# Experts of a mixed transformer step: 96 slots in plain fp32 over four column groups, in place of 128 slots in three split passes

## The reference

```
logits = (x @ w_router)                       # 8 experts
top_v, top_i = top_k(logits, 2); top_w = softmax(top_v)
gates = sum(one_hot(top_i, 8) * top_w[..., None], axis=1)
for e in range(8):
    y = y + gates[:, e:e+1] * ((silu(x @ we_gate[e]) * (x @ we_up[e])) @ we_down[e])
```

## Time and profile before

| | |
|---|---|
| median of three runs | 1605.54 us |
| the profiled execution's own time | 1617.21 us |
| its span, first to last instruction | 1615.4 us |
| TensorE busy | 1531.6 us, 95% |
| VectorE, ScalarE busy | 1133.4 us (70%), 977.0 us (60%) |
| mean granted clock | 0.953 of full speed |
| HBM read | 462.80 MB, 287 GB/s over the span |
| transfers of expert weights | 336 of 1 MB each |

### The profile page before, as it was taken

One profiled execution on the slowest core, in us unless ns is written; L12 is line 12 of the kernel. 1 busy time (PEld: TensorE's weight loads), 2 busy tenths in 40 slices (PEclk: granted clock), 3 DMA queues, 4 the chain that ended last, 5 costly groups with the idle time before them and its releaser, 6 DMA issues.

```text
span 1615.4 us, 23144 instructions
## 1 busy us (share of the span) xinstructions
PE 1531.6 (95%) x8380; PEld 1282.7 (79%) x8380; DVE 1133.4 (70%) x1260; ACT 977.0 (60%) x1131; POOL 30.5 (2%) x62
## 2 busy tenths in 40 slices
PE   7798699999797899999999999999999999999996
PEld 4755689999784878888888888888888888888885
DVE  1431634444514489989988989889989989988893
ACT  1422543344414367768777777777777777877771
POOL 0030000000030000000000000000000000000000
PEclk7898799999797899999999999999999999999997
DMA  9564567777543369989989989989989999998960
GB/s 346 196 215 141 176 242 274 275 275 247 176 158 110 116 227 361 365 327 360 363 326 357 373 316 365 365 317 359 369 313 375 365 337 345 363 371 312 363 247 28
DMA packets 210286, 464.99 MB, mean 288 GB/s; under 512 B 9226, under 2 KB 51892, under 8 KB 195892
## 3 DMA queue, kind: packets, MB, share of 16 engines
q1 hardware_dynamic: 208324, 462.80, 79.2%
q10 hardware_dynamic: 1904, 1.41, 0.3%
HBM read 462.80 MB, written 1.38 MB: 287 GB/s over the span
## 4 chain that ended last, share of the span: by engine, by line
PE 93%; DVE 4%; ACT 2%; issue 1%; DMA 0%; SPq 0%; DVEq 0%; ACTq 0%
PE ps L1515 13%; PE ps L1517 13%; PE ps L1516 13%; PE ps L1536 6%; PE ps L1538 6%; PE ps L1537 6%; PE ps L1272 5%; PE ps L1273 4%; PE ps L1274 4%; PE ps L1237 3%; PE ps L1482 2%; PE ps L1473 2%; PE ps L1283 2%; PE ps L1525 2%; PE ps L1215 1%; PE ps L1247 1%
## 5 line engine op out<-in xcount | busy, mean ns | idle before, releaser
L1036 DVE TENSOR_TENSOR low<-ring,high 128x1024 fp32r<-128x1024 f32 x672 | 795.5, 1222 | 78.4 <-ACT high L732 55.0
L732 ACT ACTIVATE high<-ring 128x1024 fp32r<-128x1024 f32 x672 | 697.5, 1061 | 163.3 <-PE ps L1517 105.1
L1515 PE MATMUL ps<-high,xg 128*128 128x512 f32 x896 | 358.7, 400 | 0.0
L1517 PE MATMUL ps<-high,xg 128*128 128x512 f32 x896 | 351.4, 392 | 0.0
L1516 PE MATMUL ps<-low,xg 128*128 128x512 f32 x896 | 348.2, 389 | 0.0
L828 DVE TENSOR_TENSOR low<-ring,high 128x1024 fp32r<-128x1024 f32 x102 | 121.2, 1222 | 153.1 <-ACT high L582 153.1
L1272 PE MATMUL ps<-hx,high 128*128 128x256 f32 x640 | 184.0, 288 | 28.9 <-DVE hx L869 13.5
L1517 PEld LDWEIGHTS ps<-high,xg 128*128 128x128 f32 x896 | 168.2, 188 | 39.4
L1516 PEld LDWEIGHTS ps<-low,xg 128*128 128x128 f32 x896 | 168.4, 188 | 35.5
L1515 PEld LDWEIGHTS ps<-high,xg 128*128 128x128 f32 x896 | 169.1, 189 | 32.1
L1273 PE MATMUL ps<-hx,high 128*128 128x256 f32 x640 | 182.0, 284 | 0.0
(11 more groups left out here) (200 smaller groups left out, 1294.5 us busy)
## 6 DMA issues: line engine op xcount, KB each, us to landing
ring<-in_moe_w_gate SPq DMA_DIRECT2D x112, 1024.0 KB, 7.1
ring<-in_moe_w_up SPq DMA_DIRECT2D x112, 1024.0 KB, 7.4
ring<-in_moe_w_down SPq DMA_DIRECT2D x112, 1024.0 KB, 6.9
ring<-in_w_ada SPq DMA_DIRECT2D x48, 1024.0 KB, 11.5
ring<-in_ffn_w_gate SPq DMA_DIRECT2D x11, 1024.0 KB, 10.0
ring<-in_ffn_w_up SPq DMA_DIRECT2D x11, 1024.0 KB, 5.4
ring<-in_ffn_w_down SPq DMA_DIRECT2D x11, 1024.0 KB, 7.2
ring<-in_w_in SPq DMA_DIRECT2D x8, 1024.0 KB, 9.6
```

What stands on the lines that cost most here:

```text
L732: A(high[:, (MP0 + i) % PIECES, :], ring[:, s, half * PIECE:(half + 1) * PIECE], ACT.Copy).then_inc(high_ready, 1)
L1036: V.tensor_tensor(low[:, q, :], ring[:, n % SLOTS, half * PIECE:(half + 1) * PIECE], high[:, q, :], ALU.subtract).then_inc(low_ready, 1)
L1515: mm(ps[:, bank, :], xh, hi[:, j, :], start=kk == 0, stop=False)
L1517: last = mm(ps[:, bank, :], xl, hi[:, j, :], start=False, stop=kk == KD - 1)
```

## The change

An expert gets 96 slots, three groups of 32, and is computed in plain fp32 without splits. The stationary operand is one group of 32 slots; the moving one is 512 weight columns; four such *units* go to the four column groups of the array. Hidden columns are worked in four steps of 1024, 1024, 1024 and 512, each as two halves (`E_WIDTH` 512, 512, 512, 256). With three groups and two halves there are six units for gate and six for up, twelve matmuls for each 128 rows of input. They fill banks 0, 1 and 2. Down gives twelve again (`DOWN`): even and odd hidden rows, two output halves, three groups, in banks 3, 4 and 5.

```diff
+CAP = 96
+ROUNDS = -(-N2 // CAP)
+E_WIDTH = (512, 512, 512, 256)
+E_COL = (0, 1024, 2048, 3072)
+UNITS = (tuple((0, u, u) for u in range(4)), tuple((1, u, u) for u in range(4)), ((0, 4, 0), (0, 5, 1), (1, 4, 2), (1, 5, 3)))
+DOWN = ((0, 0, 0, 3, 0), (0, 0, 1, 3, 1), (0, 0, 2, 3, 2), (0, 1, 2, 3, 3),
+        (0, 1, 0, 4, 0), (0, 1, 1, 4, 1), (1, 0, 2, 4, 2), (1, 0, 1, 4, 3),
+        (1, 0, 0, 5, 0), (1, 1, 1, 5, 1), (1, 1, 2, 5, 2), (1, 1, 0, 5, 3))
+TURN_BANK, GATHER_BANK = 6, 0
-COMBINE_BANKS = (6, 7, 3, 2)
+COMBINE_BANKS = (6, 7, 3, 4)
```

```diff
+ESLOTS = 14
+        ering = nc.alloc_sbuf_tensor_at("ering", [128, ESLOTS, SLOT], f32, offset=ring_at)
+                    k = 512 // width
+                    for half, w in enumerate((e_gate, e_up)):
+                        src = w[one, :, j * k:(j + 1) * k, E_COL[s]:E_COL[s] + 2 * width].rearrange("o p k n -> (o p) k n")
+                        sp.dma_start(to[:, half * SLOT // 2:(half + 1) * SLOT // 2].rearrange("p (k n) -> p k n", k=k), src).then_inc(arrives, 16)
```

TensorE's part, with its first round written out for the eight experts where it was a loop:

```diff
+                    def gate_up(s, j):
+                        i = E_ITEM["gu", s, j]
+                        width = E_WIDTH[s]
+                        rows = 512 // width
+                        w = arrived_e(i).rearrange("p (t r n) -> p t r n", t=2, r=rows)
+                        for r in range(rows):
+                            kk = j * rows + r
+                            for bank, units in enumerate(UNITS):
+                                for t, u, group in units:
+                                    c, g = divmod(u, 3)
+                                    last = mm(ps[32 * group:32 * group + 32, bank, 0:width], xg[:, kk, 32 * g:32 * g + 32], w[:, t, r, c * width:(c + 1) * width],
+                                              start=kk == 0, stop=kk == KD - 1)
+                        last.then_inc(pieces_used, 1)
+                    def turn(s):
+                        width = E_WIDTH[s]
+                        pe.wait_ge(eh_ready, k * NSTEP + (s + 1))
+                        for n in range(width // 128):
+                            a = n // 2 * 256 + n % 2
+                            nc.tensor.transpose(ps[:, TURN_BANK, n * 128:(n + 1) * 128], hm[:, 0, a:a + 255:2], ident)
+                            last = nc.tensor.transpose(ps[:, TURN_BANK + 1, n * 64:(n + 1) * 64], hm[0:64, 1, a:a + 255:2], ident[0:64, 0:64])
+                        last.then_inc(ehT_done, 1)
+                    wait_xg(k + (rnd + 1))
+                    for i, (what, s, j) in enumerate(EXPERT):
+                        if what == "gu":
+                            gate_up(s, j)
+                        else:
+                            down(s, j)
+                        if i + 1 == GATE_UP_END[0]:
+                            pe.wait_ge(Y_ready, k + (rnd + 1))
+                            combine(e)
+                            pe.wait_ge(acc_ready, k * 4 + (4 * rnd + 4))
+                            turn(0)
+                        elif what == "d" and s < NSTEP - 1 and j == 2 * E_WIDTH[s] // 256 - 1:
+                            turn(s + 1)
+                            if s + 1 == NSTEP - 1:
+                                gather(e + 1)
+                if rnd == 0:
+                    for e in range(NE):
+                        expert(e)
+                else:
+                    with pe.Fori(0, NE) as e:
+                        expert(e)
```

ScalarE takes silu in two parts (banks 0 and the first half of bank 2) and one of the two transposed blocks, VectorE multiplies in two parts and takes the other block, and neither splits anything. The six output parts of odd hidden rows are added on VectorE after ScalarE has copied two banks of even ones:

```diff
+            def add_Y(n):
+                dve.wait_ge(Y_even_ready, n)
+                V.tensor_copy(Y[64:96, 512:1024], ps[96:128, 3, :]).then_inc(Y_moved, 1)
+                dve.wait_ge(Y_moved, n)
+                for odd, half, g, bank, j in DOWN:
+                    if odd:
+                        y = Y[32 * g:32 * g + 32, 512 * half:512 * (half + 1)]
+                        last = V.tensor_tensor(y, ps[32 * j:32 * j + 32, bank, :], y, ALU.add)
+                last.then_inc(Y_ready, 1)
```

More of the change, by code:

```diff
@@ L47 @@
 FSTEPS = FF // FC
-EC = 512
-ESTEPS = FE // EC
 SLOTS = 7
@@ L482, in rest @@
                     load(e, i)
             def first_of_next(e, k):
-                for i in range(SLOTS):
-                    before = i + SLOTS * (PER_EXPERT[i] - 1)
-                    sp.wait_ge(low_ready, k * E_PIECES + (MP0 + 2 * (before + 1)))
+                for i in range(E_FIRST):
+                    sp.wait_ge(pieces_used, k * E_ITEMS + (MP0 + E_ITEMS + before_in_slot(i)))
                     load(e, i)
@@ L495, in experts @@
                 rest(NE - 1, rnd)
[L497 to L501, removed]
+            for i in range(E_FIRST):
+                if E_SLOT[i] < SLOTS:
+                    n = MOE0 + E_SLOT[i] - SLOTS
+                    if n >= N0:
+                        n -= SLOTS
+                    free(sp, n)
+                else:
+                    sp.wait_ge(pieces_used, MP0)
                 load(0, i)
@@ L506, in _ @@
             with sp.If(more > 0):
-                first_of_next(0, NE - 1)
-                experts(1)
+                for rnd in range(1, ROUNDS):
+                    first_of_next(0, NE * rnd - 1)
+                    experts(rnd)
             sp.wait_ge(y_first_ready, 1)
@@ L769, in expert @@
[L769 to L777, removed]
-                    take_Y()
[L779 to L789, removed]
@@ L1028, in _ @@
             mixer(1)
-            def split_e(k, a, z):
-                for i in range(a, z):
-                    n, half = divmod(i, 2)
-                    q = (MP0 + i) % PIECES
-                    dve.wait_ge(high_ready, k * E_PIECES + (MP0 + i + 1))
-                    V.tensor_tensor(low[:, q, :], ring[:, n % SLOTS, half * PIECE:(half + 1) * PIECE], high[:, q, :], ALU.subtract).then_inc(low_ready, 1)
-            split_e(0, 0, AHEAD)
             dve.wait_ge(logits_done, 1)
@@ new lines, in down @@
+                    def down(s, i):
+                        w = arrived_e(E_ITEM["d", s, i]).rearrange("p (r n) -> p r n", r=2)
+                        c, n = divmod(i, E_WIDTH[s] // 256)
+                        if i == 0:
+                            pe.wait_ge(ehT_first_ready, k * NSTEP + (s + 1))
+                            pe.wait_ge(ehT_last_ready, k * NSTEP + (s + 1))
+                        for odd, half, g, bank, group in DOWN:
+                            u = 3 * c + g
+                            h = (hT_first[:, 2 * n + odd, 32 * u:32 * u + 32] if u < 4 else hT_last[:, 2 * n + odd, 32 * (u - 4):32 * (u - 4) + 32])
+                            last = mm(ps[32 * group:32 * group + 32, bank, :], h, w[:, odd, 512 * half:512 * (half + 1)],
+                                      start=(s, i) == (0, 0), stop=(s, i) == (NSTEP - 1, 2 * E_WIDTH[s] // 256 - 1))
+                        last.then_inc(pieces_used, 1)
```

263 lines of the change are left out of this document (107 added, 156 removed).

## The result

The kernel after the change takes 1630.88 us (median of 4 runs, 1628.38 to 1638.16) against 1605.06 for the kernel before (4 runs, 1604.23 to 1608.98), measured beside each other: a ratio of 1.0163, with a 95% interval of 1.0126 to 1.0201. The forecast was 1573, so the change is slower by 25.8 us where 32 us less were expected. The profiled execution took 1629.55 us, with a span of 1627.7.

What follows compares the result with a forecast made beforehand. TensorE alone was taken to bound the expert stage: 120.9 us per expert against 125.87 gave -39.8, start -0.3, end +7.9, total -32 us, so 1573. The forecast by itself ranged 1561 to 1586, with rivals 1559 to 1622.

Steps and rivals of the forecast that it cites:

- Gather, combine, transposes: TensorE's small work per expert: gather 3.5 us, combine 3.3, 28 transposes 3.3 (1.6 to 3.3).
- changes of array layout: Joints where TensorE enters or leaves four column groups: eight per expert at 0.1 us more each, 0.8 (0.4 to 1.6).
- The streams: Gate, up and down matmuls of an expert: 107.9 us against 115.2, with narrow steps at 0.214 us.
- rival A: Narrow load and matmul pairs in the last gate/up step don't come fast enough, so slower: 1618 at the middle; chance 0.2.
- The waits: TensorE waiting for activation and additions: 1.9 us before turn(0), 0.1 each at turn(1) and turn(2); 2.1 per expert (0 to 4).
- The gather: The gather of an expert moves 96 columns, not 128: between 2.6 and 3.5 us, taken as 3.5.
- The transfers: Weight transfers need 114 to 117 us per expert, so the queue stays hidden behind TensorE, by some 4 us.
- rival B: Weight transfers become the bound, below 364 GB/s: 1573 to 1598, or 1613 at 350 GB/s; chance 0.15.
- C: The four column groups run one after another, over 4000 us, or an expert exceeds 96 rows, some 1900; chance 0.03.
- The start: Before the first expert: some 2 us saved ahead of the router, 1.29 waiting for PgT copies; together -0.3 (-2 to +2).
- The end: After the last down: TensorE idle 5.6 us, then the combine at the lower clock, +3.5 (0 to 3.5); together +7.9.
- The round written out: TensorE's experts as some 18,000 instructions in a row: fetching costs 0, at most 1 us per expert.

Runs made afterwards that it cites:

- experiment 1: Kernel after the change, with all hidden transposes in the 128-row form, unused rows zero: 1585.72 us, 0.9864 of the kernel before.
- experiment 2: Kernel after the change, with each turn's 128-row transposes all ahead of its 64-row ones: 1589.85 us, 0.9885 of the kernel before.
- experiment 6: Kernel before the change, with every second hidden transpose in the 64-row form, so computing less: 1648.17 us, 1.0233 of the kernel before.
- experiment 4: Kernel after the change, with TensorE's first round of experts as a hardware loop again: 1640.46 us, 1.0184 of the kernel before.
- experiment 3: Kernel after the change, with turn(0) waiting for two of the four additions, the first down item for the others: 1617.51 us, 1.0067 of the kernel before.
- experiment 5: Kernel after the change, with all transposes of 128 rows and turn(0) waiting for two additions only: 1574.64 us, 0.9771 of the kernel before.
- experiment 7: Kernel after the change, with 128-row transposes, turn(0) waiting for two additions, and PgT awaited only before the first combine: 1572.15 us, 0.9764 of the kernel before.

## Why the prediction was wrong, step by step

**The step that failed** is in "Gather, combine, transposes": "There are again 28 transposes, half of them with 64 rows: 1.6 to 3.3, taken as 3.3." Fewer rows were taken to mean at most the old time, and below it the range went down to half; above it nothing. Measured at the full clock are 8.05 us (28 by 0.288), 4.75 more. It was a size outside its own range, from a mechanism that the step missed: TensorE was to change its form at each of the 28. The next step did price changes of array layout, at 0.1 more each, but counted eight joints and not these 28. Experiment 1 parts the 4.75: with one form the same transposes take 4.05, so 4.0 are the alternation, and the rest are the joints between turns and streams, which the forecast had in another term. With the 0.1 that the gather loses behind a 64-row transpose, the alternation costs 4.1 us per expert (125.99 against 121.87) and 33 us in all, before anything that the clock adds.

A row of the trace before would have told, in part. Outside the experts two 128-row transposes, a 64-row one and a 128-row matmul follow each other, in the timeline of TensorE of the kernel before:

```profile
546.30 0.38 PE L1402 MATMUL ps<-cst,arena 128*128 128x128 f32 x2
546.61 0.27 PE L1403 MATMUL ps<-cst,arena 64*128 64x64 f32 x1
546.81 0.38 PE L1215 MATMUL ps<-ones,sq 128*128 128x1 f32 x2
```

The 64-row one starts some 0.2 us after the one before it (the pair of L1402 has 0.38, one has 0.28, so the second starts at about 546.40), and the next instruction 0.20 after it. At 0.2 each, 28 transposes take 5.6 us: half of the error would have stood in the sum, and the upper bound at least there. The Trainium skill (TensorEngine Tiling (Array Packing), Key Properties) has the rule: "Changing tiling mode (not just tile) drains the TensorE", and it lists 128x128 and 64x128 as different modes. Experiments 2 and 6 agree with it, at 0.17 us per change in an alternating run. The prediction did not weigh this rule in the step on the transposes.

**The clock**, at nothing per expert in the forecast: 1.35 us in the experts of 127.34 and 2.7 in those of 128.66 (the gate/up matmuls have 73.50 and 74.53 where 72.35 is the least, the transposes 8.25 and 8.55 where 8.05), some 2 on average, 16 us in all. How it hangs on the other two causes, by the experts in which the clock fell:

| | idle before turn(0) | transposes | experts with a dip |
|---|---|---|---|
| after | 1.48 | alternating | 8 of 8 |
| experiment 4 | 1.55 | alternating | 7 of 8 |
| experiment 3 | 0.28 | alternating | 5 of 8 |
| experiment 1 | 1.48 | all 128 rows | 2 of 8 |
| experiment 2 | 1.48 | grouped | 1 of 8 |
| experiment 6 | none | alternating | 0 of 8 |
| experiments 5, 7 | 0.28 | all 128 rows | 0 of 8 |

With both, the clock fell in 15 experts of 16; with one of them and little or none of the other, in none to five of eight. This is seen in one profiled execution of each kernel; why it falls in one expert and not in the next, in the same code, stays open.

**What was right, or nearly.** *The streams*: gate/up and down together, up to the next instruction's start, 72.35 + 36.64 = 108.99 us, forecast 107.9 + 0.8 for joints. Narrow steps: 48 records of 256 columns in 2.59 to 2.61 us, 0.216 for four; forecast 0.214. So a load and matmul pair comes every 0.054 us, and rival A, with a chance of 0.2, is refuted. *The waits*: 1.48 us before turn(0), put down to the additions, forecast 1.9; with the combine and its joint 5.20, forecast 3.3 + 1.9. The last 24 down records before turn(1) and turn(2), which VectorE's product releases, take 2.80 up to the first transpose, before turn(3) 2.69: 0.11 more, forecast 0.1 each. *The gather*: 3.74, forecast 3.5 and up to 3.5; it follows a 64-row transpose, and in experiment 1, where it doesn't, it has 3.64. The 96 columns in place of 128 save nothing. *The transfers*: no wait, share 0.91, and in experiment 5 365 GB/s asked for and 357 to 368 drawn, by stretches of 125 us; rival B, with a chance of 0.15, is refuted. So is C, as four wide records take 0.429 us together. The 358 GB/s of the Trainium skill (DMA: Bandwidth & Descriptors, Where 436 GB/s comes from), which the forecast had set aside, are passed by 2.5% where 367 were drawn.

Per expert the errors are 4.75 for the transposes with their joints, 2.0 for the clock, 0.24 for the gather and 0.1 for the streams, their other joints and the waits that lie in them: 7.1, which is 128.0 less 120.9, and 57 us over eight.

**Start and end.** The start came to +1.2 (forecast -0.3, between -2 and +2): the wait for PgT has 1.42. The end came to about +4.5 (forecast +7.9). Its wait was sized well, 6.15 against 5.6, +5.0 over before. The 3.5 for the clock didn't add: the clock was low (16 records in 5.66 us, in the loop 3.72), but from the start of the combine to the norm behind it (L1215) there are 9.49 us, against 9.91 before. VectorE's timeline shows where it went: its last addition ends 6.39 us after the combine's start, against 4.45 before, but then it stands 1.24 us where it stood 3.61, both put down to nothing that the profile shows. Why that idle time shrank wasn't tried. Together with the 57 this makes 55 of the 58 us between forecast and result.

**The range.** The forecast by itself was said to reach from 1561 to 1586. Its own bounds reach further on either side: with waits, joints and start at their upper bounds it comes to 1597. Even that is 34 us short of 1631, so what failed was the missing cost and not the choice within the bounds.

**The round written out**: 0 against the kernel before was right, but not because there is nothing to it (experiment 4).

The likeliest case was right in its bound, its streams, its waits and its transfers. Experiments 5 and 7 come to its 1573 (1574.64, 1572.15) with two and three small edits, but one of these takes away 1.2 us per expert that the forecast had counted in, which happens to cover what else it had too low. What it had no rival for was a cost in the instructions that shrank.

## What to carry to other kernels

Price a small instruction by the instructions around it: one that does less but is of another form than its neighbours can cost more than the one it replaces, and the order in which the forms come is then worth more than their size. Put all of one form together, or pad to the common form (zeros in unused rows cost nothing here). When a wait stands before a group of banks, wait for those that the next instruction writes and no others: here that was worth the 1.2 us of idle time, and some of the dips with it.

## What the runs showed of the hardware

- Between stationary blocks of 128 and of 64 rows each change costs TensorE 0.17 us beyond the 0.117 of a transpose, at the full clock; alternating, every transpose pays it (0.288 each, in both kernels). Eight of one form take 1.16 us with what follows, four and four 1.29, alternating 2.30.
- The granted clock can fall to 0.5 with TensorE marked busy for all of the stretch: in experiment 3 it fell in five experts of eight after 0.28 us of idle time and alternating transposes, in experiment 5 never after the same 0.28 us and transposes of one form, in experiment 6 never with alternating transposes and no idle time.
- A hardware loop whose body has some 2,300 TensorE instructions stood 1.04 to 1.54 us at each jump back (experiment 4), though the same code in a straight line, some 18,000 in a row, shows no such idle time at a DMA share of 0.91 to 0.96.
- Loads of 32 columns with matmuls of 256 columns come every 0.054 us a pair in four column groups, half of what the densest run of the kernel before had.
- The transfers held 366 to 368 GB/s over most stretches of 125 us (share 0.95 to 0.96) in experiment 5.
